# Applying an RMSNorm's token factor at the eviction behind the matmul, and moving the chunk level masks from GpSimd to VectorE, in a one-core hybrid decoder layer

## The reference

```python
def _rmsnorm(x, g):
    y = xf * lax.rsqrt(jnp.mean(xf * xf, axis=-1, keepdims=True) + EPS)
    return (y * g)
...
    x = x + (g_a * br_a + g_b * br_b) @ w_o
    hf = jax.nn.relu(_rmsnorm(x, norm_ffn) @ w_up)
    x = x + (hf * hf) @ w_down
    x = x + jax.nn.sigmoid(_rmsnorm(x, norm_ple) @ w_ple_gate) * (p_i @ w_ple)
```

## Time and profile before

| | us |
|---|---|
| median of three runs (lowest, highest) | 2886.86 (2875.97, 2893.18) |
| profiled execution | 2887.79 |
| its span | 2885.7 |
| TensorE busy | 2734.3 (95%) |
| VectorE busy | 1667.8 (58%) |
| ScalarE busy | 1194.6 (41%) |
| GpSimd busy | 126.0 (4%) |
| granted clock, mean | 0.962 |

### The profile page before, as it was taken

One profiled execution on the slowest core, in us unless ns is written; L12 is line 12 of the kernel. 1 busy time (PEld: TensorE's weight loads), 2 busy tenths in 40 slices (PEclk: granted clock), 3 DMA queues, 4 the chain that ended last, 5 costly groups with the idle time before them and its releaser, 6 DMA issues.

```text
span 2885.7 us, 57764 instructions
## 1 busy us (share of the span) xinstructions
PE 2734.3 (95%) x22780; PEld 2538.7 (88%) x22780; DVE 1667.8 (58%) x2866; ACT 1194.6 (41%) x1680; POOL 126.0 (4%) x105
## 2 busy tenths in 40 slices
PE   6999999999999999999999999989999999999897
PEld 5888887788888788888889999989999999999896
DVE  5766776666776766776534555554444444445654
ACT  3544454444454444454324333344433533522333
POOL 0101111101111101111100000000000000000000
PEclk8999999999999999999899999999999999999998
DMA  5533333333333333232336676545655665565553
GB/s 163 137 89 85 80 86 87 85 87 83 80 86 87 85 87 85 78 96 77 87 88 187 183 217 180 163 125 162 170 163 160 169 165 160 164 170 160 153 134 104
DMA packets 699657, 361.57 MB, mean 125 GB/s; under 512 B 43905, under 2 KB 698531, under 8 KB 698659
## 3 DMA queue, kind: packets, MB, share of 16 engines
q1 hardware_dynamic: 699598, 360.74, 46.0%
HBM read 346.12 MB, written 14.59 MB: 125 GB/s over the span
## 4 chain that ended last, share of the span: by engine, by line
PE 81%; DVE 11%; issue 3%; ACT 2%; DMA 1%; SPq 0%; DVEq 0%; ACTq 0%
PE bank L612 80%; DVE wl L1634 2%; DVE sd L1622 1%; PE bank L640 1%; DVE nrm L1314 1%; DVE yc L1314 1%; DVE sd L1311 1%; DVE inv L1311 1%; ACT L1062 1%; DVE both L1311 1%; DVE zk L1314 1%; DMA raw<-w_in 1%; DVE xl L1311 1%; DVE sd L1317 0%; DVE wl L1308 0%
## 5 line engine op out<-in xcount | busy, mean ns | idle before, releaser
L612 PE MATMUL bank<-xh,wh 128*128 128x288 f32 (+1 forms) x3136 | 1022.5, 326 | 37.4 <-DVE xl L1311 30.2
L612 PE MATMUL bank<-xl,wh 128*128 128x288 f32 (+1 forms) x3136 | 947.5, 302 | 0.0
L612 PE MATMUL bank<-xh,wl 128*128 128x288 f32 (+1 forms) x3136 | 946.0, 302 | 0.0
L612 PEld LDWEIGHTS bank<-xh,wh 128*128 128x128 f32 x3136 | 607.8, 194 | 82.6 <-issue 35.2
L612 PEld LDWEIGHTS bank<-xl,wh 128*128 128x128 f32 x3136 | 609.9, 194 | 7.7
L612 PEld LDWEIGHTS bank<-xh,wl 128*128 128x128 f32 x3136 | 608.8, 194 | 0.0
L1308 DVE TENSOR_TENSOR wl<-raw,wh 128x2048 fp32r<-128x2048 f32 x206 | 472.2, 2292 | 214.0 <-ACT wh L1006 214.0
L1006 ACT ACTIVATE wh<-raw 128x2048 fp32r<-128x2048 f32 x206 | 393.3, 1909 | 429.6 <-PE bank L612 415.1
L612 PE MATMUL bank<-sbl,wh 128*128 128x288 f32 x1792 | 536.3, 299 | 0.0
L612 PE MATMUL bank<-sbh,wl 128*128 128x288 f32 x1792 | 532.7, 297 | 0.0
L612 PE MATMUL bank<-sbh,wh 128*128 128x288 f32 x1792 | 529.7, 296 | 0.9 <-DVE wl L1308 0.9
(11 more groups left out here) (283 smaller groups left out, 2848.7 us busy)
## 6 DMA issues: line engine op xcount, KB each, us to landing
raw<-w_in SPq DMA_DIRECT2D x116, 1024.0 KB, 5.8
raw<-w_up SPq DMA_DIRECT2D x64, 1024.0 KB, 6.3
raw<-w_down SPq DMA_DIRECT2D x64, 1024.0 KB, 5.8
raw<-w_rg_o SPq DMA_DIRECT2D x16, 1024.0 KB, 5.9
raw<-w_rw_o SPq DMA_DIRECT2D x16, 1024.0 KB, 6.0
raw<-w_o SPq DMA_DIRECT2D x16, 1024.0 KB, 5.9
raw<-w_ple_gate SPq DMA_DIRECT2D x16, 1024.0 KB, 6.0
s<-state_rwkv SPq DMA_DIRECT2D x32, 128.0 KB, 3.7
```

The source lines that it names most:

```text
L612: return pe.matmul(out, lhsT, rhs, start=start, stop=stop, skip_group_check=True)
```

## The change

Norms: x is multiplied by the gain alone and split into xh and xl tile by tile, right behind each unit's eviction (`gained`), and TensorE starts on the tiles at once. The factor of a token is the same for all features, so it is applied to the product instead: VectorE evicts a w_up unit as max(bank, 0) * sums, and a gate unit as bank * sums, and ScalarE goes on from there (square and copy; Sigmoid). TensorE's product over acc moves behind the sixth of the eight parts of the first unit. The two phases that evict with a split are written out unit by unit instead of as a loop.

Masks: VectorE makes the level masks inside "pairwise", the first level ahead of the signal on which "invert1a" waits, the other four behind it; `masked` is gone from GpSimd, and TensorE waits for am_ready at level 2.

```diff
                     if part == "a":
                         pe.wait_ge(tn_ready[l - 1], count)
-                        if l == 1:
+                        if l == 2:
                             pe.wait_ge(am_ready, count)
...
+                            if inside and q == PARTS - 3:
+                                inside()
...
-            norm(1)
...
-                    phase(base, xh, xl, NB, NX, (h_relu, KT * g), before, ready=(nrm_lo, 8, 1) if g == 0 else None)
+                    phase(base, xh, xl, NB, NX, (scaled, KT * g), before, ready=(nrm_lo, 8, 2) if g == 0 else None,
+                          inside=lambda: norm(1))
...
-            norm(2)
-            pe.wait_ge(pt_ready, 2)
...
+            phase(U_PLE, xh, xl, NB, NX, (scaled, 4 * KT), before, embed, ready=(nrm_lo, 8 + KT, 2), inside=lambda: norm(2))
...
+            def gained(base, gain, n):
+                for k in range(KT):
+                    act.wait_ge(x_done, n * KT + k + 1)
+                    act.activation(xh[:, k, NB:], rga[:, k, NB:], ACT.Identity, scale=par[:, k, gain:gain + 1]).then_inc(nrm_hi, 1)
+                    hi(base + k + 2, k % 2, (base + k) // 2 + 1)
...
-                    act.activation(tmp[u][:], bank[u][:, 0:NT], ACT.Relu).then_inc(h_relu, 1)
...
+            def level_masks(l0, l1):
+                n = l1 - l0
+                masks = cst[:, C_LM + (l0 + 1) * CHUNK:C_LM + (l1 + 1) * CHUNK].rearrange("p (l t) -> p l t", l=n)
+                return tt_(am[:, l0:l1], ab[:].unsqueeze(1).to_broadcast([P, n, 4, CHUNK]),
+                           masks.unsqueeze(2).to_broadcast([P, n, 4, CHUNK]), ALU.mult)
...
+                    if later:
+                        dve.wait_ge(yy_mm, 5 * p)
+                    level_masks(0, 1)
                     dve.wait_ge(ch.sem, ch.so_far())
                     tt_(tn, tn, eye, ALU.add).then_inc(tn_ready[0], 1)
+                    level_masks(1, 5).then_inc(am_ready, 1)
...
+            def gained(base, gain, n):
+                for k in range(KT):
+                    evict = residual(base, (n * KT, 0 if n == 0 else KT))
+                    evict(k, k % 2, k // 2)
+                    dve.wait_ge(nrm_hi, 8 + (0 if n == 0 else KT) + k + 1)
+                    stt(xl[:, k, NB:], rga[:, k, NB:], par[:, k, gain:gain + 1], xh[:, k, NB:].bitcast(F32),
+                        ALU.mult, ALU.subtract).then_inc(nrm_lo, 1)
+                    lo(base + k + 2, k % 2)
...
+                    dve.wait_ge(unit_done, base + k + 1)
+                    stt(tmp[u][:], bank[u][:, 0:NT], 0.0, sums[:, NB:], ALU.max, ALU.mult).then_inc(scaled, 1)
...
-            masked(0)
             samples(0)
             with pool.Fori(1, KT) as p:
-                masked(p)
                 samples(p)
```

More of the change, by code:

```diff
@@ L916, in _, with phase @@
             step(KT, "gb", True)
-            def phase(base, hi, lo, first, last, read, before=None, extra=None, start=2, ready=None):
+            def phase(base, hi, lo, first, last, read, before=None, extra=None, start=2, ready=None, inside=None):
                 def one(k, u):
@@ L950, in _ @@
                 if kind == "up":
-                    phase(base, xh, xl, NB, NX, (h_relu, KT * g), before, ready=(nrm_lo, 8, 1) if g == 0 else None)
-                    before = (h_relu, KT * (g + 1))
+                    phase(base, xh, xl, NB, NX, (scaled, KT * g), before, ready=(nrm_lo, 8, 2) if g == 0 else None,
+                          inside=lambda: norm(1))
+                    before = (scaled, KT * (g + 1))
                 else:
@@ L964, in _ @@
             done.then_inc(pt_mm, 1)
-            norm(2)
-            pe.wait_ge(pt_ready, 2)
             def embed(k, u):
+                if isinstance(k, int) and k == 0:
+                    pe.wait_ge(pt_ready, 2)
                 pe.wait_ge(wcol_in[u], 8 * (k - u) + 16)
@@ L1251, in _ @@
             phase(U_RWO, split_merged)
-            phase(U_WO)
-            act.wait_ge(x_done, KT)
+            def gained(base, gain, n):
[3 more added lines that the diff above has]
+                    hi(base + k + 2, k % 2, (base + k) // 2 + 1)
+            gained(U_WO, GFFN, 0)
             norm(1, NT)
-            norm_split(1, NT, xh)
             n = 0
@@ L1258, in _, with hidden @@
                 base = U_FFN + n * KT
[L1260 to L1264, removed]
-                    act.activation(tmp[u][:], bank[u][:, 0:NT], ACT.Relu).then_inc(h_relu, 1)
-                    act.wait_ge(h_relu, KT * g + k + 1)
+                def hidden(k, u, i, g=g):
+                    act.wait_ge(scaled, KT * g + k + 1)
                     act.activation(tmp[u][:], tmp[u][:], ACT.Square).then_inc(h_sq, 1)
@@ L1271, in _ @@
                 if kind == "up" and g == 0:
[L1272 to L1275, removed]
+                    hi(base + 2, 0, base // 2 + 1)
+                    hidden(0, 0, 0)
+                    hidden(1, 1, 0)
+                    hi(base + 3, 1, base // 2 + 1)
+                    phase(base, hidden, start=2)
+                elif n == 7:
+                    gained(base, GPLE, 4)
                 else:
@@ L1278, in _ @@
                 n += 1
-            act.wait_ge(x_done, 5 * KT)
             norm(2, NT)
-            norm_split(2, NT, xh)
             def ple_gate(k, u, i):
[L1284 to L1288, removed]
+                act.wait_ge(scaled, 4 * KT + k + 1)
+                act.activation(tmp[u][:], tmp[u][:], ACT.Sigmoid).then_inc(sg_ready, 1)
+            hi(U_PLE + 2, 0, U_PLE // 2 + 1)
+            ple_gate(0, 0, 0)
+            ple_gate(1, 1, 0)
+            hi(U_PLE + 3, 1, U_PLE // 2 + 1)
+            phase(U_PLE, ple_gate, start=2, ahead=False)
             for b in range(4):
@@ L1327, in _, with norm_inv @@
             lo(1, 1)
-            def norm(k, width, gain, split):
+            def norm_inv(k, width):
                 first = NX - width
@@ L1344, in norm @@
                 dve.wait_ge(rms_inv, 4 * k + 4)
+            def norm(k, width, gain, split):
+                first = NX - width
+                norm_inv(k, width)
                 if k == 0:
@@ L1768, in _ @@
             dve.wait_ge(x_done, 5 * KT)
-            norm(2, NT, GPLE, (xh, xl))
+            norm_inv(2, NT)
             def embed(k, u, i):
+                dve.wait_ge(unit_done, U_PLE + k + 1)
+                tt_(tmp[u][:], bank[u][:, 0:NT], sums[:, NB:], ALU.mult).then_inc(scaled, 1)
                 dve.wait_ge(sg_ready, k + 1)
@@ L1781, in _ @@
             dve.memset(acc, 0.0)
-            phase(U_PLE, embed, ahead=False)
+            lo(U_PLE + 2, 0)
+            embed(0, 0, 0)
+            embed(1, 1, 0)
+            lo(U_PLE + 3, 1)
+            phase(U_PLE, embed, start=2, ahead=False)
             dve.wait_ge(x_done, 6 * KT)
@@ L1794, in _ @@
                 pool.memset(view, value).then_inc(init_done, 1)
[L1796 to L1803, removed]
             def samples(p):
```

29 lines of the change are left out of this document (18 added, 11 removed).

## The result

The changed kernel takes 2812.86 us (2810.13 to 2817.79), the kernel before 2881.97. The ratio on record is 0.9741, 95% interval 0.9715 to 0.9766, which is 75 us of 2886.9 (the two medians alone are 69 apart). Forecast were 35.5 us less, 2852, with 2826 as the lower end.

What follows compares the result with a forecast made beforehand. TensorE, busy 95% of the span, was taken as the bound, leaving only its waits and low-clock time to win. 15.5 + 10.5 + 7.5 + 2 = 35.5 us off 2887.8 gave 2852, range 2826 to 2869.

Steps and rivals of the forecast that it cites:

- Norm 1: First inner norm, between w_o and w_up: TensorE starts without the scaling pass and its wait on xl; 15.5 us saved.
- The wait of 0.3: First inner norm: wl of the fourth unit ends near 1907.1, needed at 1906.9, so a wait of 0.3 us.
- Norm before the gate: First gate unit: closing product 12 us earlier after a new 3.5 us wait on wcol; 10.5 us saved after clock loss.
- w_up evictions, table loads: 64 w_up units' evictions move to VectorE, and Sigmoid's gate-phase table loads go from seven to one: nothing gained or lost.
- The masks: Loop: masks move from GpSimd to VectorE, zk comes 0.5 us earlier in each of 15 passes; 7.5 us saved.
- the middle between 1.6 and 3.5: Loop: VectorE's loss per pass to GpSimd's five early instructions, bounded at 1.6 and 3.5 us, taken as 2.5.
- TensorE's first wait grows: Loop: inv is ready 0.5 us later than in the kernel before, so TensorE's wait for it lengthens.
- The clock: Loop: a shorter second wait may save low-clock time behind it; 2 us taken, between -5 and 15.
- Rival 2: In the loop, VectorE hardly held up, both waits shrink 2.8 us a pass together, no clock falls: 2820, chance 0.12.
- Rivals 1, 3 and 4: Early GpSimd work cancels masks' gain, 2862 (0.20); norm's wait only moves, 2875 (0.05); w_up eviction chain overruns, 2910 (0.04).

Runs made afterwards that it cites:

- norms_only: Changed kernel with the masks put back on GpSimd, so only the two inner norms differ from the kernel before: 2863.20 us, ratio 0.9913.
- late_samples: Changed kernel with GpSimd's five other instructions held until TensorE's product of the first inversion level is done: 2803.56 us, ratio 0.9711.
- hold_samples: Changed kernel with GpSimd's five other instructions held until ScalarE has copied ab: 2845.39 us, ratio 0.9866.
- masks_only: Kernel before with only the masks moved to VectorE: 2838.89 us, ratio 0.9818.
- after_fill: Changed kernel with 14 and 12 unread matmuls ahead of TensorE's waits for inv and sigw, in a free bank: 2822.96 us, ratio 0.9782.
- before_fill_late: Kernel before with 20 unread matmuls a pass ahead of the wait for sigw alone, in a free bank: 2855.19 us, ratio 0.9897.
- masks_twice: Changed kernel with VectorE making the four later level masks twice: 2856.83 us, ratio 0.9894.

## Why the prediction was wrong

*Norm 1* (15.5): right. The first unit is done 6.9 us after the last w_o unit (predicted 6.9), the first scaled eviction starts 11.9 behind it (12.3). The wait of 0.3 did not appear.

*Norm before the gate* (10.5): right in each link. wcol is the new wait, 3.86 us (3.5), the product comes 11.7 us sooner against its phase's end (12), and the clock falls behind the wait (1.7 us lost; 1 to 2).

*w_up evictions, table loads* (0): no sign against it: norms_only measured -25 for all of the norms' part, with 7 to either side, and 26 were forecast.

*The masks* (7.5): VectorE gains as forecast, but both sizes were off. From the start of wl to the start of inv<-ab it is 6.14 us (546.85 to 552.99), before 4.34 (562.15 to 566.49): VectorE lost 1.8 to the early five, not 2.5. The undisturbed way from inv<-ab to the end of zk took 3.60, not 4.1. So zk came 1.66 sooner, not 0.5. I had taken the middle between 1.6 and 3.5 with the argument that turns come by either way; the row lies near the lower bound, because beside wl it was GpSimd that waited. Its copy into dg took 1.23 us there, and 0.22 alone (late_samples):

```profile
552.81 0.22 POOL L1856 COPY dg<-ar 128x32 f32<-128x32 f32 x1
```

The Trainium skill, "SBUF — State Buffer", section "Who interferes with whom", says that the order of issue decides which of the two blocks. That the trace shows GpSimd losing beside wl and VectorE beside the short instructions of hold_samples is in keeping with it.

That also turned the step "TensorE's first wait grows": inv came sooner, not 0.5 later, and that wait fell from 1.9 to 1.5. Both waits together gave 19.5 us where I had 7.5: 12 of the 38.5 us that were missing.

*The clock* (+2, between -5 and 15): this is the step that failed most. 48.0 - 19.5 = 28.5 us of the loop's gain are in neither wait, and masks_only's busy time is 28.9 less. The runs put them on the clock: 15 falls behind the two waits became none, filling the waits alone gives 37 and 30, and one more mask instruction takes back 44 for 18.5 of waits. I had the row for it, used it for the gate, and let it count for 2 us in the loop, where one such fall stands in every pass. By my own sum the wait would have fallen from 2.5 to 2.0, not to 1.2, and the clock would perhaps have fallen behind that too; so the second error hangs on the first and then outweighs it.

*Rival 2*, 2820, came nearest. Two of its conditions came true: both waits shrink, and the clock falls no more behind them. The third, that VectorE is hardly held up, did not: it lost 1.8 us. And its 42 us were waits alone (2.8 a pass); measured were 48, of which 1.3 a pass are waits and the rest is clock. That its number is near is luck. Rivals 1, 3 and 4 did not happen.

Open is what pulls the clock down in the stretches that are left in the loop. In the changed kernel one of them reads 0.79, and no wait of TensorE stands in the 30 us ahead of it. No experiment was made on it, though it grew and shrank with changes made elsewhere: read in steps of 1 us, the time at the lower level from 142 to 1490 us is 154 us in the kernel before, 85 in the changed one, 99 in after_fill and 65 in before_fill_late.

```profile
592.00:600.00 8.00, 8.00 (x56) 7.01 (x56) 1.98 (x9) 2.96 (x7) 0.00 (x0) 0.79 0.37 99
```

## What to carry to other kernels

Look at the granted clock behind each wait of a kernel that TensorE bounds, and price the wait by both. Here going from 17.8 to 36.3 us of sigw waits (masks_twice) brought 23.3 us of slower matmuls with it, while waits of 1.2 and 1.5 us cost their length alone. A change that takes a wait from one kind to the other is worth far more than the difference. Count the falls over all passes, as one pass misleads: waits of the same 2.3 us had one behind them in half of the passes and not in the others. Unread matmuls ahead of the wait show quickly whether there is clock to win, but here they won more than the falls behind that wait had cost, so they do not measure it. Where a cost is bounded from both sides, carry both ends through to the waits and the clock behind them before taking the middle.

## What the hardware showed that was not expected

Work that nobody reads made a kernel faster: 300 matmuls of 200 columns, 20 a pass ahead of one wait, took 37.2 us, and the kernel was 30 us shorter. The same filler ahead of shorter waits made the other kernel 12 us slower.

Behind waits of 1.2 and 1.5 us the clock read 1.00 in every pass; behind 1.9 it fell in 5 of 15 passes (the kernel before), behind 2.27 in 7 of 14 (hold_samples) and behind 2.47 in 11 of 14 (masks_twice). The Trainium skill, "TensorE: Matmul & The Clock Gate", section "A second HAM failure mode: psum-queue depth-cycling", tells of a bf16 kernel that cycles through PSUM banks, in which frequent short idle times between groups of matmuls make the clock swing between its two levels; the longer of these waits agree with that, the shorter ones do not show it. In before_fill_late the clock fell behind 3 of the 15 waits of 1.9, as here, where 16 small matmuls took 1.10 us and not the 0.68 of the changed kernel:

```profile
558.34 1.10 PE L612 MATMUL bank<-inv,both 64*64 64x64 f32 x16 [1.90 <-DVE inv L1319]
```
